# SGU block of a streaming encoder step: spatial weights and bias loaded by the GpSimd queue, spatial mix one u chunk later with two buffers, low parts made by VectorE

## The reference, cut to what matters

```python
def sgu_mixer(x, w_in, b_in, ln_g, ln_b, w_s, b_s, w_out):
    L = min(T, SGU_CHUNK)                      # 128 for the prompt, 16 for a running stream
    z = jax.nn.gelu(x @ w_in + b_in, approximate=False)
    u, v = jnp.split(z, 2, axis=-1)            # 3072 features each
    v = layer_norm(v, ln_g, ln_b)
    w = jnp.tril(w_s[:, :L, :L])               # 4 groups of 128 x 128
    vg = v.reshape(B, N, L, SGU_GROUPS, SGU_GROUP_DIM)
    mixed = jnp.einsum('gts,bnsgc->bntgc', w, vg) + b_s[:, :L].T[:, :, None]
    y = (u * mixed.reshape(B, T, SGU_HALF)) @ w_out
    return y, v
```

## Time and profile before

| | us |
|---|---|
| median of 3 runs | 2183.18 (2179.91 to 2185.83) |
| the profiled execution | 2180.6 |
| its span | 2178.8 |
| PE busy | 2114.6 (97%) |
| PE weight loads busy | 1931.8 (89%) |
| VectorE busy | 895.7 (41%) |
| ScalarE busy | 717.7 (33%) |
| GpSimd busy | 124.0 (6%) |

### The profile page before, as it was taken

The page is one execution under the profiler, slowest core; times in us unless marked ns, Lnnn a source line. Parts: engine busy times, 40 slices in busy tenths (PEclk is TensorE's granted clock), DMA queues, the critical chain, the costliest instruction groups (busy, mean ns, idle before and its releaser), DMA issues.

```text
span 2178.8 us, 26961 instructions
## 1 busy us (share of the span) xinstructions
PE 2114.6 (97%) x11026; PEld 1931.8 (89%) x11026; DVE 895.7 (41%) x905; ACT 717.7 (33%) x821; POOL 124.0 (6%) x143
## 2 busy tenths in 40 slices
PE   7999999999999999999999999979899989999998
PEld 6999988877689999888999998868888879999987
DVE  4433433535553343335343433435644353434333
ACT  4332322343433233223333332323443233333322
POOL 0000000103100000000000000000333000000000
PEclk9999999999999999999999999989999999999999
DMA  6344343434433434344434343443433334343342
GB/s 198 121 129 126 124 136 118 152 121 160 144 124 124 131 119 135 117 135 135 135 116 135 117 143 131 140 146 126 136 108 115 135 107 135 116 134 119 131 134 88
DMA packets 216606, 283.02 MB, mean 130 GB/s; under 512 B 10144, under 2 KB 159136, under 8 KB 216544
## 3 DMA queue, kind: packets, MB, share of 16 engines
q1 hardware_dynamic: 210432, 260.39, 37.1%
q0 software_dynamic: 6112, 21.73, 3.0%
HBM read 274.23 MB, written 7.86 MB: 129 GB/s over the span
## 4 chain that ended last, share of the span: by engine, by line
PE 87%; DVE 3%; issue 2%; ACT 2%; DMA 2%; POOL 2%; SPq 1%; DVEq 0%; POOLq 0%; ACTq 0%
PE bank L1284 16%; PE bank L1283 16%; PE bank L1285 16%; PE bank L1264 10%; PE bank L1265 10%; PE bank L1266 10%; PE bank L1307 2%; PE bank L1308 2%; PE bank L1311 2%; DMA raw_sb<-ffn_w_up 1%; ACT whi_sb L433 1%; PE bank L1295 1%; DVE wlo_sb L761 1%; DMA raw_sb<-sgu_w_in 1%; POOL v_sb L1231 1%
## 5 line engine op out<-in xcount | busy, mean ns | idle before, releaser
L1283 PE MATMUL bank<-xhi_sb,whi_sb 128*128 128x384 f32 x2176 | 730.1, 336 | 0.0
L1284 PE MATMUL bank<-xlo_sb,whi_sb 128*128 128x384 f32 x2176 | 728.0, 335 | 0.0
L1285 PE MATMUL bank<-xhi_sb,wlo_sb 128*128 128x384 f32 x2176 | 727.8, 334 | 0.0
L761 DVE TENSOR_TENSOR wlo_sb<-raw_sb,whi_sb 128x2048 fp32r<-128x2048 f32 x114 | 261.6, 2295 | 445.5 <-ACT whi_sb L433 445.4
L589 ACT ACTIVATE whi_sb<-raw_sb 128x2048 fp32r<-128x2048 f32 x112 | 215.0, 1919 | 628.4 <-PE bank L1285 628.4
L1283 PEld LDWEIGHTS bank<-xhi_sb,whi_sb 128*128 128x128 f32 x2176 | 409.5, 188 | 0.2
L1284 PEld LDWEIGHTS bank<-xlo_sb,whi_sb 128*128 128x128 f32 x2176 | 409.3, 188 | 0.2
L1285 PEld LDWEIGHTS bank<-xhi_sb,wlo_sb 128*128 128x128 f32 x2176 | 409.2, 188 | 0.0
L906 DVE TENSOR_TENSOR wlo_sb<-raw_sb,whi_sb 128x2048 fp32r<-128x2048 f32 x112 | 256.7, 2292 | 326.7 <-ACT whi_sb L589 326.7
L433 ACT ACTIVATE whi_sb<-raw_sb 128x2048 fp32r<-128x2048 f32 x114 | 218.1, 1913 | 423.8 <-PE bank L1266 382.4
L1266 PE MATMUL bank<-whi_sb,hlo_sb 128*128 128x512 f32 x720 | 280.2, 389 | 0.0
(11 more groups left out here) (188 smaller groups left out, 1643.7 us busy)
## 6 DMA issues: line engine op xcount, KB each, us to landing
raw_sb<-ffn_w_down SPq DMA_DIRECT2D x64, 1024.0 KB, 5.1
raw_sb<-ffn_w_gate SPq DMA_DIRECT2D x60, 1024.0 KB, 5.3
raw_sb<-ffn_w_up SPq DMA_DIRECT2D x60, 1024.0 KB, 5.3
raw_sb<-sgu_w_in SPq DMA_DIRECT2D x24, 1024.0 KB, 5.2
raw_sb<-gla_w_in SPq DMA_DIRECT2D x12, 1024.0 KB, 5.4
raw_sb<-sgu_w_out SPq DMA_DIRECT2D x12, 1024.0 KB, 5.1
raw_sb<-ffn_w_gate SPq DMA_DIRECT2D x8, 512.0 KB, 3.8
raw_sb<-ffn_w_up SPq DMA_DIRECT2D x8, 512.0 KB, 4.9
```

Of the source, the lines that this page charges most:

```text
L761: dve.tensor_tensor(lo_part, raw[:, n % 2], hi_part.bitcast(F32), ALU.subtract).then_inc(w_lo, 1)
L1283: pe.matmul(out, whi[:, slot, cols], xhi[:, k, :], start=k == 0, stop=False)
L1284: pe.matmul(out, whi[:, slot, cols], xlo[:, k, :], start=False, stop=False)
L1285: mm = pe.matmul(out, wlo[:, slot, cols], xhi[:, k, :], start=False, stop=k == DK - 1)
```

## The change

In words, engine by engine:

- SP issues none of the small DMAs. POOL issues the weight DMAs and one DMA for the bias of 128 positions, between bias row 2 and the gain and shift rows of groups 0 and 1. POOL then copies the bias to the other places of its tile (`bs_out`) before the power.
- PE mixes chunk i-1 between the columns of chunk i, and the last mix follows the last chunk. Before, the first mix stood amid the first columns of chunk 1.
- The mix has two buffers: `mixed` for even chunks, the space of the bias rows for odd ones (`mixed_at`).
- VectorE makes the low parts of the products, behind the products of the same chunk; POOL keeps the shifts alone. Bias add, product and low part of chunk i-1 stand behind the weight's low part of chunk i+1, the gains of a group in odd i instead of even.
- ScalarE normalises the next group ahead of the rounding of the products in even i, instead of behind the GELU in odd i.
- VectorE makes the weight's low part of u chunk 1 behind the variance instead of ahead of the last statistics.

The diff:

```diff
--- before.py
+++ after.py
@@ -262,6 +262,7 @@
         bias_in = [sem(f"bias_in{i}") for i in range(2)]
         ln_in = [sem(f"ln_in{i}") for i in range(2)]
         bs_in = sem("bs_in")
+        bs_out = sem("bs_out")
         v_biased = sem("v_biased")
         v_act = sem("v_act")
         v_stat = sem("v_stat")
@@ -311,6 +312,10 @@
             else:
                 gla_before = sum(kind == "gla" for kind, _, _ in plan[:b])
                 eng.wait_ge(v_mm, (NT - 1) * (gla_before + g - 1) + t + 1)
+
+        def mixed_at(i, j):
+
+            return mixed[:, j, :] if i % 2 == 0 else bias_rows[:, j, 0:TOK]
 
         def v_at(g, t):
 
@@ -400,25 +405,10 @@
                     load_out(b, by_k(a["gla_w_out"][layer // 2]))
                 if kind == "sgu":
                     w_in = by_k(a["sgu_w_in"][layer // 2])
-                    w_s, b_s = a["sgu_w_s"][layer // 2], a["sgu_b_s"][layer // 2:layer // 2 + 1]
                     for g in range(VG):
                         for i in range(2):
                             load(n0 + 2 * g + i,
                                  w_in[:, 4 * i:4 * i + 4, HALF + g * BANK:HALF + (g + 1) * BANK], i, BANK)
-                        if g == 1:
-                            sp.wait_ge(ws_zero, 1)
-                            sp.dma_start(w_rows[:, 0], w_s.rearrange("g t s -> t g s")).then_inc(ws_in, 16)
-                            for c in range(dec_batch):
-                                at = slice(c * dec_seq, (c + 1) * dec_seq)
-                                sp.dma_start(w_rows[at, 1, :, at], w_s[:, 0:dec_seq, 0:dec_seq].rearrange(
-                                    "g t s -> t g s")).then_inc(ws_in, 16)
-                            for t in range(NP):
-                                sp.dma_start(b_spatial[:, :, tok(t)], b_s.to_broadcast([P, SPATIAL, P]))\
-                                    .then_inc(bs_in, 16)
-                            for c in range(dec_batch):
-                                at = slice(seq + c * dec_seq, seq + (c + 1) * dec_seq)
-                                sp.dma_start(b_spatial[:, :, at], b_s[:, :, 0:dec_seq].to_broadcast(
-                                    [P, SPATIAL, dec_seq])).then_inc(bs_in, 16)
                     for i in range(UC):
                         load(n0 + 2 * VG + i, w_in[:, :, i * WIDE:(i + 1) * WIDE], i % 2)
                     load_out(b, by_k(a["sgu_w_out"][layer // 2]))
@@ -721,7 +711,7 @@
                         for j in range(2):
                             c = 2 * i + j
                             act.wait_ge(u_prod, c + 1)
-                            act.activation(uhi[c // DK][:, c % DK, :], mixed[:, j, :], ACT.Copy).then_inc(u_hi, 1)
+                            act.activation(uhi[c // DK][:, c % DK, :], mixed_at(i, j), ACT.Copy).then_inc(u_hi, 1)
 
                     boundary(b, first_out)
                     act.wait_ge(const_in, 32)
@@ -731,10 +721,12 @@
                         hi(n0 + 2 * g + 3)
                     act.wait_ge(ln_moved, 1)
                     normalise(0)
-                    normalise(1)
                     for i in range(UC):
                         if i > 0:
                             hi(n0 + 2 * VG + i + 1)
+                        if i % 2 == 0 and i // 2 + 1 < VG:
+                            normalise(i // 2 + 1)
+                        if i > 0:
                             round_u(i - 1)
                         for j in range(2):
                             c = 2 * i + j
@@ -743,8 +735,6 @@
                                 act.wait_ge(u_prod, c - 1)
                             act.activation(u_act[:, j, :], banks[U_BANKS[i % 2] + j][:, 0:TOK], ACT.Gelu,
                                            bias=u_bias[:, c:c + 1]).then_inc(u_gelu, 1)
-                        if i % 2 and i // 2 + 2 < VG:
-                            normalise(i // 2 + 2)
                     round_u(UC - 1)
                     out_chunks(b)
             b = NB - 1
@@ -1055,7 +1045,8 @@
                         for t in range(NT):
                             add_bias(g, t)
                         stats(g - 1)
-                        lo(n0 + 2 * g + 3)
+                        if g < VG - 1:
+                            lo(n0 + 2 * g + 3)
                     stats(VG - 1)
                     dve.wait_ge(v_stat, NT * VG)
                     for t in range(NT):
@@ -1063,6 +1054,7 @@
                            .then_inc(ln_aggr, 1)
                     dve.wait_ge(ln_aggr, NT)
                     dve.tensor_scalar(ln_var[:, :], ln_mean_var[:, :, 1], LN_EPS, None, ALU.add).then_inc(ln_eps, 1)
+                    lo(n0 + 2 * VG + 1)
                     dve.wait_ge(ln_pow, 1)
                     dve.scalar_tensor_tensor(ln_shift[:, :], ln_mean_var[:, :, 0], -1.0, ln_rstd[:, :],
                                              ALU.mult, ALU.mult).then_inc(ln_moved, 1)
@@ -1079,32 +1071,44 @@
                            .then_inc(ln_first, 1)
 
                     def product_u(i):
+
+                        dve.wait_ge(mix_mm, i + 1)
+                        for j in range(2):
+                            c = 2 * i + j
+                            if i > 1:
+                                dve.wait_ge(u_lo, c - 3)
+                            dve.tensor_tensor(mixed_at(i, j), banks[6 + j][:, 0:TOK],
+                                              b_spatial[:, c * SPATIAL // HK, :], ALU.add).then_inc(mix_out, 1)
                         for j in range(2):
                             dve.wait_ge(u_gelu, 2 * i + j + 1)
                             dve.wait_ge(mix_out, 2 * i + j + 1)
-                            dve.tensor_tensor(mixed[:, j, :], mixed[:, j, :], u_act[:, j, :], ALU.mult)\
+                            dve.tensor_tensor(mixed_at(i, j), mixed_at(i, j), u_act[:, j, :], ALU.mult)\
                                .then_inc(u_prod, 1)
+                        for j in range(2):
+                            c = 2 * i + j
+                            if c == DK:
+                                dve.wait_ge(v_stored[0], 16)
+                            if c == 2 * DK:
+                                dve.wait_ge(v_stored[1], 16)
+                            dve.wait_ge(u_hi, c + 1)
+                            dve.tensor_tensor(ulo[c // DK][:, c % DK, :], mixed_at(i, j),
+                                              uhi[c // DK][:, c % DK, :].bitcast(F32), ALU.subtract).then_inc(u_lo, 1)
 
                     for t in range(NT):
                         gain_v(0, t)
                         if t > 0:
                             shift_v(0, t - 1)
                     shift_v(0, NT - 1)
-                    dve.wait_ge(bs_in, 16 * (NP + dec_batch))
+                    dve.wait_ge(bs_out, NP)
                     for i in range(UC):
                         if i > 0:
                             lo(n0 + 2 * VG + i + 1)
-                        if i % 2 == 0 and i // 2 + 1 < VG:
+                        if i % 2 and i // 2 + 1 < VG:
                             for t in range(NT):
                                 gain_v(i // 2 + 1, t)
-                        dve.wait_ge(mix_mm, i + 1)
-                        for j in range(2):
-                            c = 2 * i + j
-                            if i > 0:
-                                dve.wait_ge(u_lo, c - 1)
-                            dve.tensor_tensor(mixed[:, j, :], banks[6 + j][:, 0:TOK],
-                                              b_spatial[:, c * SPATIAL // HK, :], ALU.add).then_inc(mix_out, 1)
-                        product_u(i)
+                        if i > 0:
+                            product_u(i - 1)
+                    product_u(UC - 1)
                     out_chunks(b)
             for t in range(NT):
                 second_half(NB - 1, t)
@@ -1213,11 +1217,28 @@
                     boundary(b)
                     pool.wait_ge(w_used, n0 + 2)
                     pool.memset(w_rows[:, 1], 0.0).then_inc(ws_zero, 1)
-                    for g in range(2, VG):
+                    pool.wait_ge(v_biased, NT)
+                    load_bias(2)
+                    w_s = a["sgu_w_s"][j]
+                    pool.dma_start(w_rows[:, 0], w_s.rearrange("g t s -> t g s")).then_inc(ws_in, 16)
+                    pool.wait_ge(ws_zero, 1)
+                    for c in range(dec_batch):
+                        at = slice(c * dec_seq, (c + 1) * dec_seq)
+                        pool.dma_start(w_rows[at, 1, :, at], w_s[:, 0:dec_seq, 0:dec_seq].rearrange("g t s -> t g s"))\
+                            .then_inc(ws_in, 16)
+                    pool.dma_start(b_spatial[:, :, 0:P], a["sgu_b_s"][j:j + 1].to_broadcast([P, SPATIAL, P]))\
+                        .then_inc(bs_in, 16)
+                    load_ln(0)
+                    load_ln(1)
+                    for g in range(3, VG):
                         pool.wait_ge(v_biased, NT * (g - 1))
                         load_bias(g)
```

(30 more changed lines are left out.)

## The result

| | before | after |
|---|---|---|
| median of 4 runs, us | 2183.72 (2179.91 to 2185.83) | 2147.5 (2145.61 to 2148.24) |
| the profiled execution, us | 2180.6 | 2147.22 |
| its span, us | 2178.8 | 2145.4 |
| the u stage, us | 137.75 | 118.76 |

The ratio is 0.9838 [0.9827, 0.985]: 36 us by the medians, 33.4 by the two spans (the profiled execution of before lay 3 us under its median). The time forecast was 2149. (The u stage runs from the first column matmul to the first matmul of the output weights.) The profiled execution of after reached the block 1.06 us later than that of before: POOL zeroed the tile of spatial weights at 1432.50 instead of 1431.44.

A forecast was written before the change was run, and what follows sets the result against it. PE was taken as full nearly everywhere, so time could come only from its waits and low clock in the SGU block. Terms of -14.4 and -18.8 us summed to -33.2 us, giving 2149 us, range 2143 to 2160.

The forecast's parts named there:

- Term 1: First stall of the SGU block: small DMAs leave SP's queue, so the idle 11.6 us and low clock go, -14.4 us.
- Term 2: u stage: earlier start and reordered loop make it 119.0 us instead of 137.75, -18.8 us.
- A: u stage: PE alone bounds it, since the products don't wait for POOL's shift; 2147 us, chance 0.12.
- B: u loop: round trip over the engines is 1 to 3 us a pair longer than worked out; 2158 us, chance 0.2.
- D: u loop: odd chunk's trip so long that PE waits and its clock falls every pair; slower, 2193 us, chance 0.03.
- E: POOL's queue: spatial weights come so late that the first stall moves to PE's transposes; 2163 us, chance 0.03.
- C: Weight loads: transfers collide on the shared DMA engines whoever issues them, so landing stays long; 2154 us, chance 0.06.

The follow-up runs named there:

- Run 1: Kernel before with only the small loads moved from SP to POOL, with the bias copies; u stage as before: 2166.77 us, ratio 0.9935.
- Run 7: Changed kernel with all 19 small DMAs on POOL's queue, the 64 byte bias pieces among them, and no bias copies: 2147.02 us, ratio 0.9837.
- run 9: Changed kernel with its ten DMAs (nine weight, one bias) at the old place on SP's queue, bias copies still on POOL: 2152.07 us, ratio 0.9859.
- run 11: run 8 with VectorE's low part of u chunk 1 behind the shift of the mean instead of ahead of it: 2145.11 us, ratio 0.9826.
- run 6: Changed kernel with each of POOL's five shifts (groups 1 to 5) added twice: 2163.51 us, ratio 0.9919, u stage 135.19 us.
- run 3: Run 1 with the low parts of u on VectorE behind each product, in the old order with one buffer: 2153.37 us, ratio 0.9865.
- run 4: Changed kernel with the low parts of u back on POOL; new order and two buffers stay: 2147.73 us, ratio 0.9843.
- run 5: Changed kernel with one mixed buffer for even and odd chunks: 2147.56 us, ratio 0.9842.
- run 10: run 4 with one mixed buffer, so low parts of u on POOL and only the new order left: 2147.95 us, ratio 0.9838.
- run 12: run 8 with the shifts of groups 1 to 5 on VectorE, so POOL does no arithmetic in the u loop: 2146.52 us, ratio 0.9835.
- run 8: Changed kernel with ScalarE's normalising of group 1 moved from ahead of the first GELU of u to behind the next weight rounding: 2146.35 us, ratio 0.9838.

## Why the prediction was right

**Term 1** said -14.4 us. The u stage starts at 1514.80 instead of 1528.37; with the 1.06 us by which this execution came later, that is 14.6. Run 1 alone gives 15.1. The idle 11.6 us are gone and so is the low clock behind them. POOL's 14 issues took 7.7 us, just under the 8 to 13, and each copy 0.6 of the 0 to 1.2. One step was right for part of the reason: I put the 9.23 us of the late load to the small pieces alone. Run 7's 13.9 us show that they can do that. But in before, as in run 9, both slots had come free while SP stood, and two loads went out together; run 9, without the small pieces of the bias, still had 8.3 us. Run 9's expectation rested on that step and failed with it. The landing of before's loads of 1445.70 and 1446.9:

```profile
DMA to landing us min/median/max: 9.2/9.9/10.6
```

The prediction also left out a part of the stall: SP stood for the zeroed tile before its first small DMA, 4.0 us from the end of the low part that freed the slot (1428.01) to 1431.99, ahead of the 13.7 us of issues. Both went with the move, so the sum did not depend on it. That low part in before:

```profile
1425.72 2.29 DVE L761 TENSOR_TENSOR wlo_sb<-raw_sb,whi_sb 128x2048 fp32r<-128x2048 f32 x1 [1.01 <-ACT whi_sb L433]
```

**Term 2** said 119.0 us for the u stage, and it is 118.76. Its parts:

| | forecast, us | measured, us |
|---|---|---|
| mix 0 begins, after the stage's start | 13.4 | 13.31 |
| wait at mix 0 | 1.0 | 0.64 |
| u chunk 3 begins, after the stage's start | 30.0 | 29.97 |
| wait before u chunk 3 | 1.4 | 1.23 |
| PE's own work and the small rests | 116.6 | 116.89 |
| trip, even and odd half | 7.6 + 11.9 | 7.5 + 11.9 |

That the power stands for the low part is shown by 2.85 us in after against 0.89 in run 11; that the products stand for the shift, by 3.62 against 1.02 us and by run 6's 6.90. The Trainium skill (SBUF — State Buffer, section Who interferes with whom) calls the ports that VectorE shares with GpSimd an exclusive lock; these three rows agree with it. Only the size of the first products was off (two to three microseconds were forecast), at no cost: the start of the shift to ScalarE's rounding, on which the sum rests, took 3.96 us (1554.10 to 1558.06) against the 3.93 used.

What the prediction did not separate is which edit of the loop matters. It worked out the new loop as one; runs 3, 4, 5 and 10 show that the new order, with the later mix, would have done without the other two edits.

**The rivals.** A fell: the products do wait. The time alone could not have told, since 2147.5 is nearer A's 2147 than 2149, and the wait costs little: the trip is 0.1 us a pair over PE's need, and run 12, without the wait, takes no less time than run 8. B fell: the trip is 19.41 us a pair, 0.1 under the forecast, where B needed 1 to 3 over it. Run 6 shows that its arithmetic holds: 3.3 us more a pair made the stage 16.4 us longer. D would have needed such a longer trip, and none came. E fell: bias row 3 waited for VectorE, not for the issues, and PE did not wait at the transposes.

C fell in after, where the load issued at 1437.99, amid POOL's DMAs, and its neighbours landed within 5.6 us. The Trainium skill (DMA: Bandwidth & Descriptors, section Issuing engines are not separate DMA queues) says that another issuer saves only the issue time, since all queues run on the same 16 DMA engines. The trace agrees with the second half: run 9's loads and rows stretched one another to 8.3 and 10.3 us, and run 7's load on SP's queue took 13.9 us beside small pieces on POOL's. The first half falls short here: beside run 9, the other issuer let the loads go out one by one, the first 9.0 us earlier, of which 5.0 were issues. So C's mechanism is there in run 7, and what hides it is slack: 7.0 us of ScalarE's waiting reach no engine that sets the time.

## What to carry to other kernels

Before moving a small DMA, look at what stands behind it in its queue: a train of issues ahead of a weight load costs its own time and any wait at its head, then lets the next loads bunch up and land late together. Where an elementwise step of a loop waits until another engine has freed its buffer, moving that step one iteration later may replace both a second buffer and a move of work to another engine. And after such a change, compare the loop's trip over all engines with the busiest engine's need: here they differ by 0.1 us a pair, so the next microsecond put on the trip is paid in full, as run 6 shows.

## What the runs showed that I had not expected

One weight load beside eight DMAs of small pieces on another queue took 13.9 us to land in run 7; two issued together took 8.3 and 10.3 in run 9; one at a time takes 5.1. A power on 128x3 elements took 2.85 us instead of 0.89 because it began 0.18 us after a VectorE low part of 2.28. VectorE did the shift of three tiles in 1.89 us, where POOL took 3.50 and held VectorE's products for 2.6 of them.
